# Scan stage of a two-block transformer kernel: the output-gate piece is projected before the second forget gate, and the scan of a head starts one piece later

## The reference, cut to what matters

```python
def hgrn2_mixer(h_lat, h_ctx, w_in, lb, norm_g, w_o, need_ctx_out):
    def project(h):
        q, v, g, f_fwd, f_bwd = jnp.split(h @ w_in, splits, axis=-1)
        return heads(silu(q)), heads(v), g, heads(f_fwd), heads(f_bwd)
    q_c, v_c, g_c, ff_c, fb_c = project(h_ctx)
    o_c, s_fwd, s_bwd = bidirectional(q_c, v_c, ff_c, fb_c, zero, zero)
    q_l, v_l, g_l, ff_l, fb_l = project(h_lat)
    o_l, _, _ = bidirectional(q_l, v_l, ff_l, fb_l, s_fwd, s_bwd)
    return (rms_norm(o_l, norm_g) * silu(g_l)) @ w_o      # only the latent tokens are read out
```

## Time and profile before

| | before |
|---|---|
| median of three runs | 3602.86 us (3601.08 to 3602.98) |
| the profiled execution | 3599.17 us |
| its span in the trace | 3597.4 us |
| mean granted PE clock | 0.974 of full speed |
| PE busy | 3328.5 us, 93% of the span |
| DVE / ACT / POOL busy | 1747.3 / 1273.6 / 399.4 us |

### The profile page before, as it was taken

How to read it: one execution, slowest core, us unless ns; L and a number is a source line. 1 busy time by engine, 2 the same in 40 slices (tenths; PEclk the granted TensorE clock), 3 DMA queues, 4 the chain that set the end, 5 groups by cost and what they waited for, 6 DMA issues and landing times.

```text
span 3597.4 us, 42857 instructions
## 1 busy us (share of the span) xinstructions
PE 3328.5 (93%) x17064; PEld 2756.1 (77%) x17064; DVE 1747.3 (49%) x2602; ACT 1273.6 (35%) x1965; POOL 399.4 (11%) x400
## 2 busy tenths in 40 slices
PE   3888878999999999997999999999989999999898
PEld 3777757888887778776788878887768788877686
DVE  3666667755533676765533334343333333433333
ACT  2444443212123465554322233333332333333322
POOL 1011001000001253533000000001100000011000
PEclk7999999999999999998999999999999999999999
DMA  5322213665621211111333322222223222222132
GB/s 175 86 68 64 68 47 112 193 195 191 194 91 47 64 48 48 48 42 43 101 94 95 93 96 70 76 74 79 69 67 100 91 81 72 69 83 76 53 97 85
DMA packets 107974, 318.75 MB, mean 89 GB/s; under 512 B 28160, under 2 KB 29568, under 8 KB 107264
## 3 DMA queue, kind: packets, MB, share of 16 engines
q1 hardware_dynamic: 107776, 316.00, 28.3%
HBM read 313.86 MB, written 2.10 MB: 88 GB/s over the span
## 4 chain that ended last, share of the span: by engine, by line
PE 80%; DVE 7%; ACT 5%; POOL 4%; issue 3%; DMA 1%; SPq 0%; DVEq 0%; ACTq 0%
PE bank L914 20%; PE bank L916 20%; PE bank L915 20%; PE bank L919 3%; PE bank L921 3%; PE bank L920 3%; PE bank L1108 1%; DVE tmp L1560 1%; PE bank L1127 1%; PE bank L1137 1%; POOL hg_d L1994 1%; ACT L1165 1%; PE bank L1009 1%; POOL hg_d L1995 1%; PE bank L982 1%
## 5 line engine op out<-in xcount | busy, mean ns | idle before, releaser
L914 PE MATMUL bank<-h_high_lat,w_high 128*128 128x512 f32 x2752 | 1136.0, 413 | 84.5 <-DVE h_low_ctx L1566 34.6
L1514 DVE TENSOR_TENSOR w_low<-w_raw,w_high 128x1024 fp32r<-128x1024 f32 (+2 forms) x440 | 537.3, 1222 | 1125.2 <-ACT w_high L1185 1123.8
L916 PE MATMUL bank<-h_high_lat,w_low 128*128 128x512 f32 x2752 | 1082.6, 393 | 0.0
L915 PE MATMUL bank<-h_low_lat,w_high 128*128 128x512 f32 x2752 | 1082.5, 393 | 0.0
L1185 ACT CAST w_high<-w_raw 128x1024 fp32r<-128x1024 f32 (+2 forms) x440 | 451.1, 1027 | 1335.0 <-PE bank L916 858.8
L914 PEld LDWEIGHTS bank<-h_high_lat,w_high 128*128 128x128 f32 x2752 | 523.0, 190 | 195.7 <-issue 63.6
L916 PEld LDWEIGHTS bank<-h_high_lat,w_low 128*128 128x128 f32 x2752 | 522.4, 190 | 113.1
L915 PEld LDWEIGHTS bank<-h_low_lat,w_high 128*128 128x128 f32 x2752 | 524.6, 191 | 79.3 <-issue 8.2
L1526 DVE SCALAR_TENSOR_TENSOR ada_product<-w_raw,c_rows 128x1024 f32<-128x1024 f32 x192 | 246.0, 1281 | 65.5 <-DMA w_raw<-in_ada_w_dram 53.8
L1951 POOL TENSOR_TENSOR rstd<-rstd,square 128x512 f32<-128x512 f32 (+1 forms) x42 | 64.8, 1544 | 1496.9 <-ACT square L1166 1496.6
L919 PE MATMUL bank<-h_high_ctx,w_high 128*128 128x256 f32 x800 | 225.6, 282 | 0.0
(11 more groups left out here) (244 smaller groups left out, 4285.4 us busy)
## 6 DMA issues: line engine op xcount, KB each, us to landing
w_raw<-in_w_in_dram SPq DMA_DIRECT2D x176, 512.0 KB, 3.5
w_raw<-in_ada_w_dram SPq DMA_DIRECT2D x88, 512.0 KB, 3.9
w_raw<-in_ffn_in_dram SPq DMA_DIRECT2D x88, 512.0 KB, 3.6
w_raw<-in_w_ada_dram SPq DMA_DIRECT2D x48, 512.0 KB, 4.5
w_raw<-in_hg_in_dram SPq DMA_DIRECT2D x40, 512.0 KB, 3.5
w_raw<-in_ffn_out_dram SPq DMA_DIRECT2D x32, 512.0 KB, 3.6
w_raw<-in_qkv_dram SPq DMA_DIRECT2D x24, 512.0 KB, 3.6
w_raw<-in_proj_ret_dram SPq DMA_DIRECT2D x16, 512.0 KB, 3.5
```

What stands on the lines that cost most here:

```text
L914: e.matmul(lat_b, a, h[:, k, :], start=start, stop=False)
L915: e.matmul(lat_b, a, l[:, k, :], start=False, stop=False)
L916: done = e.matmul(lat_b, b, h[:, k, :], start=False, stop=stop)
L1514: e.tensor_tensor(w_lo[n % 2][:, 0:w], raw[slot][:, 0:w], w_hi[n % 2][:, 0:w].bitcast(F32), ALU.subtract).then_inc(s_lo, 1)
```

## The change

For head 0 the pieces now come in the order q, f0, g, f1, v, and for the others f0, q, g, f1, v. The mixer of a head still starts after the epilogue of f1, which is now the fourth piece (index 3). So beside the mixer of head i lie v of its own head and f0, q, g and f1 of the next. For head 7 only v is left beside the mixer, and the count of chunks given for it goes from 28 to 21.

```diff
     def hg_pieces(self, i):
         W = self.io["hg_in"]
+        q, g, f0 = (0, "hg_q", "h"), (2, "hg_g", "h"), (3, "hg_f0", "hc")
         return [lambda then, b=b, name=name, rhs=rhs: self.piece(W[b * 8 + i], KC, rhs, (name, i), then=then,
                                                                  gate=("norm", 2) if i == 0 and b == 0 else None)
-                for b, name, rhs in ((0, "hg_q", "h"), (3, "hg_f0", "hc"), (4, "hg_f1", "hc"), (1, "hg_v", "hc"), (2, "hg_g", "h"))]
+                for b, name, rhs in ((q, f0, g) if i == 0 else (f0, q, g)) + ((4, "hg_f1", "hc"), (1, "hg_v", "hc"))]
@@
         self.interleave([self.hg_pieces(i) for i in range(HG_HEADS)], [(self.hg_mixer(i), 34) for i in range(HG_HEADS)], 5 * (KC - 1),
-                        tail_chunks=4 * (KC - 1), after=2)
+                        tail_chunks=3 * (KC - 1), after=3)
```

## The result

| | before | changed |
|---|---|---|
| median of 13 runs each, on one chip | 3602.23 us (3598.43 to 3602.98) | 3608.43 us (3606.57 to 3612.15) |
| ratio of changed to before, 95% interval | | 1.0020 [1.0013, 1.0028] |
| the profiled execution, its span | 3599.17, 3597.4 us | 3608.42, 3606.6 us |

What follows compares the result with a forecast made beforehand. The prediction took each head to be bound by a chain through DVE, POOL and ACT, then by PE. Its terms, 5.44 + 0 + 0 + 1.4 + 3.0 = +9.8 us on 3602.86, gave 3612.7 us, range 3605 to 3620 us.

Steps and rivals of the forecast that it cites:

- The rival by which the slow clock costs nothing: Heads: slow clock falls into the wait or slack, or does not come; +6.8 us in all, 3609.7 us, chance 0.33.
- The lead-in, +5.44 us: Before the first mixer: all 24 matmuls of head 0's g lie on the path, +5.44 us.
- The w_low wait, 0: Ahead of q: PE's seven waits for w_low go, but nothing behind q moves up, 0 us.
- The rival by which the wait of q was what counted: Ahead of q: if the chain followed PE's start of q, 13.1 us faster, 3589.8 us, chance 0.07.
- The copy, +1.4 us: DVE: f0's context copy now stands ahead of hg_x(0) and delays the chain, +0.20 us in each of seven heads.
- the term's lower bound: DVE: if f0's context copy is absorbed, hg_a(6) starts earlier, -0.21 us a head or -1.5 us.
- g in place of f0: Beside the levels: shorter chunks only move PE's waiting, about 3.4 us at hg_a(4), 0.85 us of slack ahead of hg_a(6).
- The clock, +3.0 us: Behind the wait at hg_a(4): PE runs at 1.2 GHz, 0.6 us lost in each of five of seven heads.
- the rival by which every head pays: Heads: the slow clock costs its full price in every head; +12.9 us in all, 3615.8 us, chance 0.12.
- The end, 0: Last mixer: g of head 7 leaves a place where it was free, so its 5.44 us come back nowhere, 0 us.
- The end gets slower: Last mixer: PE idles some 9 us before v's transposes, slow clock on small matmuls adds some 2 us; 3614.7 us, chance 0.08.

Runs made afterwards that it cites:

- experiment 1: Changed kernel, but g of each head comes behind q of the next head and g of head 7 comes last: 3604.58 us, 1.0007 against before.
- experiment 6: The order of experiment 1 plus eight unused matmuls on PE ahead of hg_a(4) in heads 0 to 6: 3601.61 us, 1.0003 against before.
- experiment 2: Changed kernel with two more small reductions on DVE directly ahead of f0's context copy, for seven heads: 3609.29 us, 1.0015 against before.
- experiment 4: Changed kernel with the weight step of the first output-projection piece moved ahead of v of head 7: 3607.79 us, 1.0011 against before.
- the early casts: Order of experiment 1, with seven of eight y_lat blocks cast and projection weights prepared inside the last mixer: 3598.50 us, 0.9989 against before.
- the early gate: Order of experiment 1, with sigmoid, logarithm and running sum of the next head's f0 moved ahead of this head's hg_o: 3591.59 us, 0.9974 against before.
- both in the order of experiment 1: The early casts and the early gate together, on the order of experiment 1: 3583.79 us, 0.9952 against before.
- 11: The early casts and the early gate plus eight unused matmuls ahead of hg_a(4), on the order of experiment 1: 3582.62 us, 0.9949 against before.
- experiment 3: Changed kernel with eight unused matmuls on PE ahead of hg_a(4) in heads 0 to 6: 3604.36 us, 1.0007 against before.
- the last of the table: Kernel before, in its own order q, f0, f1, v, g, with the early casts and the early gate: 3592.20 us, 0.9973 against before.

## Why the prediction came out as it did

The direction and the main mechanism, a bare piece in the lead-in and a chain in the heads that does not follow PE, were right: the stage is 5.4 and 7.3 us longer in two executions, the medians differ by 6.2 us, and 9.8 us were forecast. The number owes something to luck: terms of both signs were missed and partly cancel. The rival by which the slow clock costs nothing (6.8 us) lies nearer to the measured time than the forecast, though its mechanism is refuted. The terms one by one:

- **The lead-in, +5.44 us: exact.** 5.45 us between the epilogues, and undone by experiment 1.
- **The w_low wait, 0: right.** The waits are gone, and no stretch but that of head 0 (44.62, before 44.77) is below 45.3 us. The rival by which the wait of q was what counted is out.
- **The copy, +1.4 us: the step that failed.** "+0.20 us in each of seven heads" took a delay on DVE to be one of the chain. The pair behind the copy started 0.36 us later and took 0.33 us less, and hg_x(6) ends where it ended before (44.32 and 44.33 us behind v). That is the case of the term's lower bound, in which PE is no longer the last ahead of hg_a(6), with -0.21 us a head; measured are -0.10 us in head 1, and 0.9 us less over the seven heads where the low clock is away (experiment 6, 400.72 against 401.61). Experiment 2 shows that more work at the same place does move the chain, by 0.63 us.
- **g in place of f0: right that the wait only moves, half right in the place.** 3.4 us of waiting were to stand at hg_a(4) and 0.85 us of slack at hg_a(6); 2.02 and 0.69 us do, and 0.98 us stand at hg_a(3). The bank that `hg_state` frees was overlooked.
- **The clock, +3.0 us: right in kind and in price per head, and the number of heads is not fixed.** 1.35 us of slower work less 0.69 us of slack cost 0.67 us a head, where 0.6 was taken from 1.72 less 0.85. Of seven heads three had it in one execution and the five forecast in the other: 2.0 and 3.4 us. All seven had it in experiment 1, four in experiment 4, none in experiment 2, behind waits of the same length. Neither the rival by which every head pays nor the one by which none does holds as a rule. The 0.44 us of head 5 came beside it unforeseen.
- **The end, 0: missed by 0.90 us.** The 56.31 us were right to the hundredth, counted from the epilogue. That the epilogue itself comes earlier once no piece follows v(7), the prediction did not ask.
- **The end gets slower: did not come.** PE's idle time grew from 4.48 to 8.36 us as it said, and the transposes took 1.51 us as before. Experiment 6 shows that a low clock in the end can cost 1.6 us, but on `hg_o` and with the shorter wait of 4.48 us, so not by the way that this rival named.

With the measured terms: 5.45 - 0.9 - 0.90 + 0.44 + 2.0 (or 3.4) = 6.1 (or 7.5) us. The first execution had 0.62 us of that back from the start of the stage, which leaves 5.5 against 5.40; the second had nothing of it back, 7.5 against 7.32. The last 0.1 to 0.2 us were not traced.

## What to carry to other kernels

Ask of a piece that is moved off the side of a serial chain what it covers at either end: in the middle it only trades one wait of PE for another, but at the start it lies bare, 5.4 us for one piece. Where a stretch keeps its length while PE's own time in it changes (45.47 and 45.49 us in the heads before), look for the chain that sets it: reordering PE's work alone won at most 0.9 us there (experiment 6), while taking work out of the chain (1.45 us a head) and filling idle slots of ACT at the end won 17 to 18 us. The order still counts for what may be taken out: in the order of before the same edit won 2.2 us in a stretch and lost 1.8 us of it in f1, because what it moved had to wait for f0. And a copy put ahead of a link of the chain costs only what the next instruction does not give back, so look whether that one was held up by another engine.

## What was not expected of the hardware

- A wait of PE of 2.02 us was followed by 1.2 GHz in 0, 3, 5 and 7 of seven heads (experiment 2, the changed kernel twice, experiment 1), and in 4 to 7 of seven in the other runs that had such a wait (experiment 4, the early casts, the early gate, and both in the order of experiment 1). It cost 0.67 us where PE had 0.69 us of slack behind it. In the kernels whose longest wait in the heads was 1.0 us (experiments 6 and 11), 1.6 us (experiment 3) or 1.9 us (the last of the table), it did not come. These are one execution each.
- A POOL instruction of 0.61 us takes up to 1.61 us beside a DVE instruction that reads two operands from SBUF, and DVE's pair 1.76 instead of 1.34 us where POOL is first. A near tie went with 0.44 us of a head, in the same head in four executions.
